# Host-packed channel-major slabs in a hybrid decoder step: wider modulation groups, a first norm in two halves, and small loads behind the first slabs

## The chip, the core and the metric

The kernel runs on one core of one Trainium2 chip. The metric is device time in microseconds (us), the median of the runs shown. The engines are named as in the profile: PE (matmul), PEld (weight load), DVE (vector), ACT (scalar), POOL, and SPq, the queue of the sync engine, which issues every DMA of this kernel in program order.

## The reference, cut to what matters

One layer of a hybrid decoder on 288 tokens (256 of a prompt, 8 samples of 4), model width 1024, everything in float32. A conditioning vector per sequence (9 of them) gives six modulation vectors of 1024 through a 1024 x 6144 weight. The modulated norm feeds two recurrent branches, which are merged, projected and added; a second modulated norm feeds a mixture of experts; a final norm ends it.

```
cs  = silu(c)                                     # (9, 1024)
mod = cs @ w_ada + b_ada                          # (9, 6, 1024)
shift1, scale1, gate1, shift2, scale2, gate2 = mod
h = rms_norm(x, norm1_w) * (1 + scale1) + shift1
proj = h @ w_in                                   # GLA q k v gate, decay rank 16, GDN q k v (conv), z, beta, a, gates
y, new_state_gla, new_state_gdn, new_state_conv = mixer(proj, states)
x = x + gate1 * (y @ w_out)
h = rms_norm(x, norm2_w) * (1 + scale2) + shift2
x = x + gate2 * moe(h)                            # 16 experts, 2 for each token, gate and up 1024x512, down 512x1024
return rms_norm(x, final_norm_w), states
```

## The kernel before, in words

All activations are kept channel-major in one SBUF arena: `xT` and `hT` are 128 partitions x 8 channel blocks x 288 tokens. Each engine runs the same hand-written `schedule` list in order, and takes from each item the part that is its own; engines meet through semaphores. The order of the list is therefore the order of the work on PE, ACT and DVE, and no engine reorders it.

1. **Head.** SPq loads constants (886 KB), the nine conditioning rows, vectors, convolution weights, x in token rows, and a dozen small tensors, and only then the first weight slab. PE turns the rows into channel-major form by transposes (L420 is the line of every matmul, L423 that of every transpose); DVE copies them out.
2. **Modulation.** `w_ada` comes in 24 slabs of 256 columns, 1 MB each. For one slab `ada` does 8 matmuls with 32-column weights and 256 moving columns, in four column groups of the array (four partial sums, two contraction blocks each); ACT copies the bank to `adaq` (L1776), and `fold` adds the four partial sums with two matmuls that have 128-column weights and 9 moving columns; DVE adds the bias (L1038). Slabs 0 to 7 (shift and scale of the first norm) come in the head, and `norm_sums` (the sums of squares of x, 8 matmuls of 288 columns) stands behind the third of them; slabs 8 to 23 stand behind steps 1, 3, ... 31.
3. **First norm and small projections.** `norm` scales and modulates all eight blocks (DVE L1047, L1056 to L1071, ACT L1797). `small` then projects the decay rank, beta and a: 8 matmuls, an ACT copy (L1803), five small matmuls.
4. **Steps 0 to 69.** Step s projects block s of 64 (8 matmuls of 128 x 128 weights and 288 columns), with the transposes, norms and convolution taps of earlier blocks. Weight slabs of 256 columns go through a ring of five 1 MB slots; SPq loads chunk n when chunk n-5 has been used. The pieces of the GLA branch stand at steps 21 to 35 (`GLA_AT`), those of GDN from step 38, and `conv_out` (24 transposes of the convolution tails to token rows) behind step 46.
5. **Output projection, second norm, router, experts.** Eight blocks of two experts each in a loop, whose weights stream from HBM in three 4 MB loads for each block; then the final norm, `y` turned back to token rows by 24 transposes, and four stores.

`ring_bank` hands out four PSUM banks in turn, `take` the other four by number; both wait until the last reader has read.

Of the kernel before, what the change touches and what calls it, by code (L numbers as in the profile page):

```python
# [22 lines left out]
P = 128  # L23
# [55 lines left out]
def constants():  # L79

    p = np.arange(P)
    parts = {"ident": np.eye(P), "ones": np.ones((P, P)), "tri": (p[:, None] <= p[None, :]) * 1.0}
# [10 lines left out]
    parts["eps"] = np.full((P, 1), EPS)  # L93
# [16 lines left out]
CONST, CONST_AT = constants()  # L110

# [37 lines left out]
def _program(nc, ctx, I, O, known):  # L149
# [26 lines left out]
    csT = carve(KD * NC9 + 32 - NC9)  # L176
    adaq = carve(CW)
    vecT = carve(NVEC)
    cst = carve(CONST.shape[1])
    rsB = carve(TOK)  # L180
    rtw = carve(KD * 20 + 12)
    rtb = carve(20)
    gs = carve(2, 32)
# [25 lines left out]
    ccT = carve(CT, 27)  # L209
    wsm = carve(KD, 32)  # L210
    raT_at = top[0]
# [7 lines left out]
    adt = carve(2, HB)  # L219
# [50 lines left out]
    xr = vB  # L270
    cbrow = carve(3072, at=persistent + RING * KD * CW)
    crow = carve(D, at=GB_at)
    csx = carve(2, D, at=vA_at + 0)
    vrow = carve(P, at=GB_at + 1024)
    cvrow = carve(P, at=GB_at + 1152)
    newconv = carve(3072, at=vA_at)

    EW = carve(3, 2, 4096, at=mixer_only)
    yrow = carve(3, D, at=mixer_only)
# [37 lines left out]
    def cols(w, c0, n=CW):  # L317
        return w[:, c0:c0 + n].rearrange("(k p) n -> p k n", p=P)

# [34 lines left out]
    for c in range(8):  # L354
        schedule += [("ada", c)] + ([("fold", c - 1)] if c else [])
        if c == 2:
            schedule.append(("norm_sums", 1))
    schedule += [("fold", 7), ("norm", 1), ("small",)]
    ADA_AT = {ADA_FIRST + ADA_STEP * i: 8 + i for i in range(16)}
    for s in range(NPROJ + 6):  # L360
        schedule.append(("step", s))
        if s == 1:
            schedule.append(("sums",))
# [7 lines left out]
        if s == CONV_OUT_AT:  # L371
            schedule.append(("conv_out",))
    schedule += [("merge",), ("wout",), ("norm_sums", 2), ("norm", 2), ("router",), ("experts",), ("final",)]

    for item in schedule:
        kind, c = item[0], item[-1]
        if kind == "ada":
            add(("ada", c), cols(I["w_ada"], CW * c))
        elif kind == "step" and c % 2 == 0 and c < NPROJ:
            add(("win", c), cols(I["w_in"], PROJ[c][2]))  # L380
        elif item == ("gla_states_read", 2):
            for i in range(4):
                add(("sgla", i), I["state_gla"][2 * i:2 * i + 2].rearrange("s h k v -> k (s h) v"))
        elif item == ("gdn_values", 2):
            for i in range(4):
                add(("sgdn", i), I["state_gdn"][2 * i:2 * i + 2].rearrange("s (h a) k v -> k (s h) a v", a=2))
        elif kind == "wout":
            for i in range(4):
                add(("wout", i), cols(I["w_out"], CW * i))
# [87 lines left out]
    def _(pe):  # L477
        PE[0] = pe

        def head():  # L480
            pe.wait_ge(*when("consts"))
            pe.wait_ge(*when("vec rows"))
            b = ring_bank("vec")
            tr(b[:, 0:NVEC], vrow[0:NVEC, :], NVEC)
            tr(b[:, 128:224], cvrow[0:96, :], 96).then_inc(mark("head_transposed", "vec ready"), 1)
            pe.wait_ge(*when("x rows"))
            for d in range(KD):
                b = ring_bank(f"x{d}")
                for m, (o, n) in enumerate(TILES):
                    last = tr(b[:, o:o + n], xr[0:n, m, 128 * d:128 * d + 128], n)  # L490
                last.then_inc(mark("head_transposed", f"x{d} ready"), 1)
            pe.wait_ge(*when("cb rows"))
            for g in range(2):
                b = ring_bank(f"cb{g}")
                for j in range(12):
                    c = 12 * g + j
                    last = tr(b[:, 24 * j:24 * j + 24], cbrow[0:24, 128 * c:128 * c + 128], 24)
# [1798 lines left out]
```

## Time and profile before

| what | value |
|---|---|
| median of 3 runs (lowest to highest) | 962.63 us (962.33 to 968.43) |
| the profiled execution's own time | 964.75 us |
| its span, first to last instruction | 962.9 us |
| mean granted TensorE clock | 0.959 |
| busy: PE, DVE, ACT, POOL | 871.8, 411.2, 261.2, 66.3 us |
| DMA | 190.64 MB, mean 198 GB/s |

The span is what the trace covers; the execution's own time is 1.9 us longer, and the median of the runs lies 2.1 us below that. A busy PE is not PE at full rate: matmuls overlap, and the granted clock is 1.0 or 0.5 of full speed from one stretch to the next.

### The profile page before, as it was taken

To read this page: it belongs to the slowest core of one execution; us is meant where nothing else is said; L and a number is where in the kernel's file an instruction comes from. 1 tells how busy PE (TensorE), PEld (TensorE's weight loads), DVE (VectorE), ACT (ScalarE), POOL (GpSimd) and SP (SyncE) were. 2 spreads that over 40 slices of the span, in tenths; PEclk is the share of its full clock that TensorE was granted. 3 is DMA by queue.
4 is the path that set the end of the run, shared out by engine and by line. 5 is a ranking of instruction groups with operands and counts; after the bars stand their busy time and mean duration, and the time that the engine had idled before them with its cause. 6 is when DMAs were issued, how large, how long until landed. Compare 5 with 4: busy or idle time off the path is not lost.

```text
span 962.9 us, 13134 instructions
## 1 busy us (share of the span) xinstructions
PE 871.8 (91%) x5070; PEld 611.5 (64%) x5070; DVE 411.2 (43%) x1038; ACT 261.2 (27%) x630; POOL 66.3 (7%) x94
## 2 busy tenths in 40 slices
PE   5889999998979899999999996794999999999994
PEld 3557777676747689878988776573555445554533
DVE  3120004647756865557447447515123222232225
ACT  3121103666732333352433421012101110111012
POOL 1000000000123100000000117310000000000000
PEclk9969999999989999999999998996999999999998
DMA  8947676523517811132113523798399999998811
GB/s 205 349 136 232 203 223 209 176 88 98 168 41 221 261 45 45 47 129 88 45 45 101 145 76 99 211 381 314 116 396 368 384 385 395 376 387 331 292 57 50
DMA packets 134414, 190.64 MB, mean 198 GB/s; under 512 B 6656, under 2 KB 90283, under 8 KB 134309
## 3 DMA queue, kind: packets, MB, share of 16 engines
q1 hardware_dynamic: 134360, 189.89, 58.1%
q8 instruction: 37, 0.61, 0.3%
q14 instruction: 17, 0.14, 0.1%
HBM read 178.93 MB, written 10.95 MB: 197 GB/s over the span
## 4 chain that ended last, share of the span: by engine, by line
PE 79%; DVE 10%; ACT 3%; issue 3%; POOL 2%; SPq 2%; DMA 1%; DVEq 0%; ACTq 0%; POOLq 0%
PE bank L420 76%; PE bank L423 3%; POOL arena L2091 1%; DMA arena<-in_w_ada 1%; DVE arena L1185 1%; DVE arena L1653 1%; DVE arena L1047 1%; SPq L2142 1%; DVE arena L1296 1%; ACT arena L1751 0%; DVE arena L1170 0%; DVE arena L1339 0%; POOL arena L2099 0%; DVE arena L1494 0%; DVE arena L1434 0%
## 5 line engine op out<-in xcount | busy, mean ns | idle before, releaser
L420 PE MATMUL bank<-arena 128*128 128x288 f32 (+9 forms) x4752 | 830.9, 394 | 72.0 <-DVE arena L1071 8.6
L420 PEld LDWEIGHTS bank<-arena 128*128 128x128 f32 (+4 forms) x4752 | 575.5, 172 | 312.1 <-issue 181.0
L1848 ACT ACTIVATE arena<-arena 128x288 f32<-128x288 f32 (+1 forms) x56 | 25.0, 447 | 154.2 <-DVE arena L1170 154.1
L423 PE MATMUL bank<-arena 128*128 128x128 f32 (+6 forms) x318 | 50.3, 291 | 14.9 <-DMA arena<-in_w_conv 7.0
L423 PEld LDWEIGHTS bank<-arena 128*128 128x128 f32 (+6 forms) x318 | 36.9, 149 | 34.5 <-issue 19.8
L1660 DVE TENSOR_TENSOR arena<-arena,bank 128x288 f32<-128x288 f32 x64 | 28.8, 455 | 29.4 <-PE bank L420 28.0
L1185 DVE SCALAR_TENSOR_TENSOR arena<-arena 128x312 f32<-128x312 f32 x72 | 39.4, 548 | 2.5
L1038 DVE TENSOR_TENSOR arena<-bank,arena 128x18 f32<-128x18 f32 x24 | 4.2, 174 | 82.7 <-PE bank L420 82.7
L1640 DVE SCALAR_TENSOR_TENSOR arena<-bank,arena 128x512 f32<-128x512 f32 x8 | 5.5, 693 | 71.4 <-ACT arena L1998 71.4
L1746 ACT ACTIVATE arena<-arena 128x288 f32<-128x288 f32 (+4 forms) x60 | 33.7, 562 | 2.0
L1881 ACT ACTIVATE arena<-bank 128x288 f32<-128x288 f32 x40 | 16.2, 405 | 54.4 <-PE bank L420 30.7
L1321 DVE TENSOR_TENSOR arena<-arena 128x512 f32<-128x512 f32 (+1 forms) x32 | 19.9, 638 | 24.1 <-PE bank L420 24.1
L1170 DVE SCALAR_TENSOR_TENSOR arena<-arena 128x288 f32<-128x288 f32 (+1 forms) x56 | 26.6, 475 | 8.5 <-ACT arena L1746 8.5
L1391 DVE TENSOR_TENSOR arena<-arena,bank 128x512 f32<-128x512 f32 (+1 forms) x26 | 17.0, 657 | 29.5 <-PE bank L420 29.5
L1744 ACT ACTIVATE arena<-arena 128x288 f32<-128x288 f32 (+4 forms) x60 | 28.2, 470 | 1.9
L1751 ACT ACTIVATE arena<-bank,arena 128x288 f32<-128x288 f32 x19 | 9.5, 500 | 68.5 <-PE bank L420 68.5
L1988 ACT ACTIVATE arena<-bank 128x512 f32<-128x512 f32 x8 | 4.8, 599 | 84.4 <-PE bank L420 84.4
L1742 ACT ACTIVATE arena<-arena 128x288 f32<-128x288 f32 (+2 forms) x57 | 25.5, 447 | 4.7 <-DMA arena<-in_cc 3.9
L1994 ACT ACTIVATE arena<-bank 128x512 f32<-128x512 f32 x8 | 4.8, 598 | 80.0 <-PE bank L420 80.0
L2091 POOL TENSOR_SCALAR arena<-arena 128x1024 f32<-128x1024 f32 x8 | 23.3, 2930 | 44.8 <-PE bank L420 44.8
L2056 POOL COPY arena<-arena 128x3 f32<-128x3 f32 x24 | 6.9, 287 | 276.9 <-ACT arena L1876 276.9
L2004 ACT ACTIVATE arena<-bank 128x512 f32<-128x512 f32 x8 | 4.8, 598 | 70.0 <-PE bank L420 70.0
(206 smaller groups left out, 466.8 us busy)
## 6 DMA issues: line engine op xcount, KB each, us to landing
arena<-in_w_in SPq DMA_DIRECT2D x36, 1024.0 KB, 6.6
arena<-in_w_exp_gate SPq DMA_DIRECT2D x8, 4096.0 KB, 14.9
arena<-in_w_exp_up SPq DMA_DIRECT2D x8, 4096.0 KB, 18.2
arena<-in_w_exp_down SPq DMA_DIRECT2D x8, 4096.0 KB, 14.6
arena<-in_w_ada SPq DMA_DIRECT2D x24, 1024.0 KB, 5.3
arena<-in_state_gla SPq DMA_DIRECT2D x4, 1024.0 KB, 6.4
out_gla_s<-arena SPq DMA_DIRECT2D x4, 1024.0 KB, 8.2
arena<-in_w_out SPq DMA_DIRECT2D x4, 1024.0 KB, 6.1
```

The costliest lines, as they stand in the source:

```text
L420: return T.matmul(out, lhsT, rhs, start=start, stop=stop)
L423: return T.transpose(out, in_, ident[0:n, 0:n])
L1170: V.scalar_tensor_tensor(sg, y, 0.0, sg, ALU.min, ALU.subtract) \
L1185: V.scalar_tensor_tensor(y, x[:, j:j + YW], wv(j), y, ALU.mult, ALU.add) \
L1321: V.tensor_tensor(Lm[0:n, hs, 0:n], LT[0:n, hs, 0:n], mid(const(f"level{lv}")[0:n, 0:n], HG), ALU.mult) \
L1391: V.tensor_tensor(X[0:n, hs, 0, 0:n], X[0:n, hs, 0, 0:n], view(6 + g), ALU.subtract) \
L1660: V.tensor_tensor(acc[:, d, :], acc[:, d, :], pm[4 + d % 4][:, 0:TOK], ALU.add).then_inc(n["added"], 1)
L1742: A.activation(dst, src, ACT.Abs).then_inc(mark(kind, event + " abs"), 1)
L1744: A.activation(dst, dst, ACT.Exp, scale=-1.0).then_inc(mark(kind, event + " exp"), 1)
L1746: A.activation(dst, dst, ACT.Ln, bias=one[0:n]).then_inc(mark(kind, event), 1)
L1848: A.activation(sg, sg, ACT.Exp).then_inc(mark("proj_by_scalar", f"sig{s3}"), 1)
L2091: G.tensor_scalar(kem2[:, s % 2, :], ke.rearrange("p a b -> p (a b)"), const("seq")[:, s:s + 1], None, ALU.mult) \
```

## The change

The host now lays every input out as the arena wants it (128 partitions, one contiguous run each), and takes the outputs in that form. On the chip:

- The head's transposes and their copies go, as do `conv_out` and the 24 transposes of `y`; the convolution tails and `y` are stored channel-major. `y` goes out in four stores of two blocks each, as the final scaling produces them.
- The conditioning, the vectors and the constants that the head needs come as one load (`first`, 427 floats in each of 128 partitions), then x; then the weight slabs begin. Four loads (`small`, `later`, `wa2`, `conv`) are issued behind the slab of step 2.
- The modulation is done in 12 groups of 512 columns, each from two 1 MB slabs that hold four contraction blocks each. The four column groups of the array now hold four different blocks of 128 output columns, so nothing is left to add up, and `fold` is one transpose. Groups 2, 0, 3, 1 come in the head (scale and shift of the first half, then of the second), `norm_sums` ahead of them; the other eight behind steps 1, 5, ... 29.
- The first norm is modulated half by half, each when its two groups are there; step 0's matmul k waits for block k. `small` moves from ahead of step 0 to behind step 2, `sums` from step 1 to step 4. The second norm is modulated in halves too, and its scales are formed earlier.
- Three router banks are taken by number; `gla_out` waits for the masked scores.

```diff
-ADA_FIRST, ADA_STEP = 1, 2
+ADA_FIRST, ADA_STEP = 1, 4
-CONV_OUT_AT = 46
+ADA_HEAD = (2, 0, 3, 1)
+ADA_ORDER = ADA_HEAD + tuple(range(4, 12))
+SMALL_AT, SUMS_AT = 2, 4
-NORM_BY_VECTOR = (2, 5)
+NORM_BY_VECTOR = (3, 7)
...
-    for c in range(8):
-        schedule += [("ada", c)] + ([("fold", c - 1)] if c else [])
-        if c == 2:
-            schedule.append(("norm_sums", 1))
-    schedule += [("fold", 7), ("norm", 1), ("small",)]
-    ADA_AT = {ADA_FIRST + ADA_STEP * i: 8 + i for i in range(16)}
+    schedule.append(("norm_sums", 1))
+    for i, c in enumerate(ADA_HEAD):
+        schedule += [("ada", c)] + ([("fold", ADA_HEAD[i - 1])] if i else [])
+        if i == 2:
+            schedule.append(("norm_half", 0))
+    schedule += [("fold", ADA_HEAD[3]), ("norm_half", 1)]
+    ADA_AT = {ADA_FIRST + ADA_STEP * i: 4 + i for i in range(8)}
...
         if kind == "ada":
-            add(("ada", c), cols(I["w_ada"], CW * c))
+            for half in range(2):
+                add(("ada", c, half), I["w_ada"][2 * c + half])
...
         def ada(c):
-            w = slot(("ada", c))
-            b = take(7 - 2 * (c % 2), f"read ada{c}")
-            for k in range(KD):
-                q = k % 4
-                last = mm(b[32 * q:32 * q + 32, 0:CW], csT[:, NC9 * k:NC9 * k + 32], w[:, k, :], k < 4, k >= 4)
+            b = take(7 - 2 * (ADA_ORDER.index(c) % 2), f"read ada{c}")
+            for half in range(2):
+                pe.wait_ge(*when(loaded(("ada", c, half))))
+                w = slot(("ada", c, half)).rearrange("p k n -> p (k n)").rearrange("p (k n) -> p k n", n=512)
+                for j in range(4):
+                    k = 4 * half + j
+                    for q in range(4):
+                        last = mm(b[32 * q:32 * q + 32, 0:P], csT[:, NC9 * k:NC9 * k + 32],
+                                  w[:, j, P * q:P * q + P], k == 0, k == KD - 1)
...
         def fold(c):
-            for j in range(2):
-                last = mm(b[:, NC9 * j:NC9 * j + NC9], adaq[:, 128 * j:128 * j + 128], FOLD[:, 0:NC9])
+            tr(b[:, 0:P], adaq[:, ADA_ORDER.index(c) % 2, :], P).then_inc(mark("ada_products", f"fold{c} ready"), 1)
...
                 for k in range(KD):
+                    if s == 0:
+                        pe.wait_ge(*when(f"h1 {k}"))
+                        pe.wait_ge(*when(f"hp1 {k}"))
                     last = mm(b[:, 0:TOK], w[:, k, 128 * j:128 * j + 128], hT[:, k, :], k == 0, k == KD - 1)
...
         def gla_out(m):
+            pe.wait_ge(*when(t + "AT"))
...
-        def conv_out():
-            for g in range(6):
-                b = ring_bank(f"cvo{g}")
-                for j in range(4):
-                    last = tr(b[0:27, 128 * j:128 * j + 128], ccT[:, 4 * g + j, :], 128)
...
+        def modulate(i, half):
+            dve.wait_ge(*when(f"A{i} {half}"))
+            dve.wait_ge(*when(f"read fold{(base + 4 * half) // 4}"))
+            dve.wait_ge(*when(f"n{i} {4 * half + 3}"))
+            V.tensor_tensor(hs, hs, AA[:, ds, 1:NC9].unsqueeze(3).to_broadcast(wide), ALU.mult)
+            V.tensor_scalar(hT[:, by_vector, 0:SEQ], hT[:, by_vector, 0:SEQ], AA[:, by_vector, 0:1],
+                            modT[:, base + by_vector, 0:1], ALU.mult, ALU.add)
+            V.tensor_tensor(hs, hs, modT[:, base + 4 * half:base + 4 * half + 4, 1:NC9].unsqueeze(3).to_broadcast(wide),
+                            ALU.add)
...
-        load(cst, I["const"], "consts")
-        load(crow[0:NC9, :], I["cc"], "c rows")
...
+        load(arena[:, first_at:first_end], I["first"], "first")
+        load(xT, I["x"], "x")
+        def later_weights():
+            load(arena[:, wsm_at:small_end], I["small"], "small weights")
+            load(arena[:, first_end:later_end], I["later"], "consts")
+            load(wa2[0:RANK + 1, :], I["wa2"], "wa2")
+            load(arena[:, convT_at:convT_at + 96 + CT * 24], I["conv"], "conv weights")
...
+            sp.dma_start(slot(name), src).then_inc(mark(f"loaded_slot{n % RING}", loaded(name), by=16), 16)
+            if name == ("win", 2):
+                later_weights()
...
-            sp.dma_start(into[:, 0:n, :].rearrange("p a (k n) -> p (a k) n", k=4 if kind == 2 else KD),
-                         wts[kind][experts].rearrange("a (k p) n -> p (a k) n", p=P)).then_inc(sem, 16)
+            sp.dma_start(into[:, 0:n, :], wts[kind][experts].rearrange("a p n -> p a n")).then_inc(sem, 16)
...
+        for d in range(0, KD, 2):
+            sp.wait_ge(*when(f"yf {d + 1}"))
+            sp.dma_start(O["y"][:, d:d + 2, :], hT[:, d:d + 2, :]).then_inc(mark("stored", f"y stored {d}", by=16), 16)
```

## Rows read from the trace of the kernel before

**Rows 1.** The page: busy time of PE, and shares of the chain that ended last.
```profile
PE 871.8 (91%) x5070; PEld 611.5 (64%) x5070; DVE 411.2 (43%) x1038; ACT 261.2 (27%) x630; POOL 66.3 (7%) x94
...
PE 79%; DVE 10%; ACT 3%; issue 3%; POOL 2%; SPq 2%; DMA 1%; DVEq 0%; ACTq 0%; POOLq 0%
```

**Rows 2.** Windows: length, busy (instructions) of PE, PEld, DVE, ACT, POOL; clock; DMA share; GB/s.
```profile
100.00:150.00 50.00, 48.33 (x272) 35.40 (x265) 3.14 (x13) 5.71 (x17) 0.33 (x2) 1.00 0.66 210
...
700.00:800.00 100.00, 97.38 (x523) 50.45 (x521) 27.42 (x51) 11.50 (x19) 0.00 (x0) 1.00 1.02 384
```

**Rows 3.** Chain that ended last, 0 to 62 us: start, length, what.
```profile
0.71 0.40 SPq L2123
...
15.78 0.43 SPq L2193
...
54.70 2.63 PE bank L420 x16
```

**Rows 4.** Timeline: PE's and DVE's part in the small projections.
```profile
57.81 17.39 PE L420 MATMUL bank<-arena 128*16 128x288 f32 x80 [0.50 <-ACT arena L1803]
...
60.18 0.19 DVE L1081 COPY arena<-bank 128x32 f32<-128x32 f32 x1 [0.74 <-PE bank L420]
```

**Rows 5.** DMA issues: KB of each, median us from issue to landing.
```profile
arena<-in_const SPq DMA_DIRECT2D x1, 886.0 KB, 4.8
...
arena<-in_gdn_A_log SPq DMA_DIRECT2D x1, 4.0 KB, 2.2
```

**Rows 6.** Windows: the ada loads, clock before step 0, in step 0, expert loads.
```profile
28.00:30.00 2.00, 1.89 (x18) 0.74 (x17) 0.18 (x1) 0.38 (x1) 0.00 (x0) 1.00 1.11 352
44.00:45.00 1.00, 1.00 (x8) 0.93 (x4) 0.00 (x0) 0.00 (x0) 0.00 (x0) 0.50 1.10 347
64.00:65.00 1.00, 1.00 (x5) 0.76 (x4) 0.00 (x0) 0.00 (x0) 0.00 (x0) 0.82 0.00 0
...
650.00:651.00 1.00, 0.00 (x0) 0.00 (x0) 0.96 (x3) 0.01 (x1) 0.00 (x0) 1.00 1.02 406
```

**Rows 7.** PE by form, 28 to 40 us: the sums of squares.
```profile
L420 PE MATMUL bank<-arena 128*128 128x288 f32 x16 | 7.1, 627 | 0.0
```

**Rows 8.** PE by form, 100 to 127 us: projections, ada, fold (two records per matmul).
```profile
L420 PE MATMUL bank<-arena 128*128 128x288 f32 x93 | 24.1, 412 | 0.0
L420 PE MATMUL bank<-arena 128*32 128x256 f32 x48 | 3.2, 384 | 0.0
L420 PE MATMUL bank<-arena 128*128 128x9 f32 x12 | 1.5, 236 | 0.0
```

**Rows 9.** Chain at 561.7 us: 128 matmuls, 32-column weights, 128 columns.
```profile
561.70 7.17 PE bank L420 x256
```

**Rows 10.** PE timeline: a fold that waits for ACT; a GLA step.
```profile
134.58 4.59 PE L420 MATMUL bank<-arena 128*128 128x9 f32 x20 [0.83 <-ACT arena L1776]
...
183.62 1.07 PE L420 MATMUL bank<-arena 128*32 128x256 f32 x16 [0.35 <-DVE arena L1220]
186.75 1.59 PE L420 MATMUL bank<-arena 128*128 128x128 f32 x8 [2.05 <-DVE arena L1237]
```

**Rows 11.** Window behind that GLA step.
```profile
188.00:190.00 2.00, 2.00 (x9) 1.71 (x9) 1.93 (x7) 1.28 (x4) 0.00 (x0) 0.50 1.08 351
```

**Rows 12.** PE by form, whole span: the transposes of the convolution tails.
```profile
L423 PE MATMUL bank<-arena 128*27 128x128 f32 x24 | 2.8, 271 | 0.0
```

**Rows 13.** Chain, second norm: eight products on DVE, then the router's matmuls.
```profile
650.04 3.04 DVE arena L1047 x8
...
655.16 2.48 PE bank L420 x16
```

**Rows 14.** Timeline, the end: eight final scalings, the last store's issue.
```profile
952.05 3.52 DVE L1722 SCALAR_TENSOR_TENSOR arena<-arena 128x288 f32<-128x288 f32 x8 [4.44 <-ACT arena L1755]
...
959.84 0.47 SPq L2250 DMA_DIRECT2D out_y_s<-arena  x1
```

**Rows 15.** PE by form, whole span: gate, up and down products, and their waits.
```profile
L420 PE MATMUL bank<-arena 128*64 128x512 f32 x768 | 172.0, 599 | 7.0 <-DVE arena L1653 7.0
```

More of the change, by code:

```diff
@@ L478, in _ @@
         PE[0] = pe
[L480 to L497, printed above, removed]
-                last.then_inc(mark("head_transposed", f"cb{g} ready"), 1)
-            b = ring_bank("c")
-            for k in range(KD):
-                last = tr(b[:, NC9 * k:NC9 * k + NC9], crow[0:NC9, 128 * k:128 * k + 128], NC9)
-            last.then_inc(mark("head_transposed", "c ready"), 1)
@@ new lines, in ada @@
+            for half in range(2):
[6 more added lines that the diff above has]
+                                  w[:, j, P * q:P * q + P], k == 0, k == KD - 1)
+                last.then_inc(mark("ada_products", used(("ada", c, half)), *([f"ada{c} ready"] if half else [])), 1)
@@ L861, in router @@
         def router():
-            pe.wait_ge(*when("router weights"))
-            pe.wait_ge(*when("router padding"))
+            pe.wait_ge(*when("consts"))
             b = ring_bank("router parts")
@@ L901, in router @@
             q = MORE * NE
-            b = ring_bank("over")
+            b = take(7, "read over")
             mm(b[0:q, 0:1], tri[0:q, 0:q], over[0:q, 0:1])
@@ L967, in experts @@
             pe.wait_ge(*when("one-hot"))
-            b = ring_bank("table")
+            b = take(5, "read table")
             q = MORE * NE
@@ L1074, in small, with norm_half @@
+        def norm_half(half):
+            scales(1, half)
+            modulate(1, half)
+        def norm(i):
+            for half in range(2):
+                for d in range(4 * half, 4 * half + 4):
+                    normed(2, d)
+                modulate(2, half)
         def small():
+            dve.wait_ge(*when("consts"))
             dve.wait_ge(*when("ra ready"))
@@ L1079, in small @@
             dve.wait_ge(*when("ba ready"))
-            dve.wait_ge(*when("adt"))
+            dve.wait_ge(*when("small weights"))
             V.tensor_copy(ba[:, 0:2, :], rb("ba")[:, 0:32].rearrange("p (a b) -> p a b", b=16))
@@ L1176, in step @@
                     x, y = xp[:, s1 % 2], yb[:, s1 % 4]
-                    dve.wait_ge(*when("read c"))
+                    dve.wait_ge(*when("conv weights"))
                     for event in y_free(s1 - 4):
@@ L1520, in wout @@
         def wout():
[L1521 removed]
+            dve.wait_ge(*when("read fold5"))
             for d in range(KD):
@@ L1799, in norm, with norm_half @@
                     .then_inc(mark("norm_by_scalar", f"hp{i} {d}"), 1)
+        def norm_half(half):
+            modulate(1, half)
+        def norm(i):
+            for half in range(2):
+                modulate(2, half)
         def small():
+            act.wait_ge(*when("consts"))
             act.wait_ge(*when("small parts ready"))
@@ L1869, in step @@
                     act.wait_ge(*when("xp zero"))
-                    act.wait_ge(*when("read cb1"))
+                    act.wait_ge(*when("conv weights"))
                     if i >= 2:
@@ L2026, in final @@
             rstd(rsB, rb("norm3")[:, 0:TOK], 1.0 / D, "norm_by_scalar", "rstd3", mid_event="read norm3")
-            for g in range(2):
-                act.wait_ge(*when(f"y{g}1 ready"))
-                A.activation(yrow[:, 1, 512 * g:512 * g + 512], rb(f"y{g}1")[:, :], ACT.Copy) \
-                    .then_inc(mark("final_by_scalar", f"read y{g}1"), 1)
         run(locals())
```

320 lines of the change are left out of this document (126 added, 194 removed).

## The prediction

> **What bounds the kernel now.** I read the page first: PE is busy 91% of the span and makes up 79% of the chain that ended last, DVE 10%, DMA 1% [rows 1]. That is an average, so the windows by stage come next. Between 100 and 150 us PE is busy 48.3 of 50 us and in the experts 97.4 of 100, at full clock in both [rows 2]: there a microsecond taken off PE is a microsecond of the span, and nothing else is. The head is different. The chain in order of time shows that the first slab of modulation weights is issued only at 15.8 us, behind everything SPq had to issue before it, although its first issue stands at 0.7; after the ada groups come the small projections, and step 0 starts when the last small product is out, at 60.2 us [rows 3, 4]. So the change can pay in three kinds: an earlier step 0, PE work taken out of the dense steps, and a shorter end.
>
> **The head: when step 0 starts afterwards.** First the loads. A 886 KB load landed 4.8 us after its issue and a 4 KB one 2.2 us [rows 5]; `first` is 219 KB, so by proportion 2.8 us, landing at 3.5. x (1.18 MB) and eight slabs (1.05 MB each) follow without a gap. The rate is the unknown: 352 GB/s for slabs in runs of 1 KB, 406 for expert weights in runs of 2 and 4 KB [rows 6]. At these two rates x lands at 6.9 or 6.4, a slab takes 2.98 or 2.58 us, the eighth lands at 30.7 or 27.0 and the ninth, step 0's own, at 33.7 or 29.6. The new runs are 8 KB, so I take the higher rate, whose row is nearer, and keep the other for the range.
>
> The Trainium skill, "DMA: Bandwidth & Descriptors", section Specifications, gives about 358 GB/s as the limit of HBM for one core; by that the eight slabs would take 23.4 us in place of 20.6 and the sum below would come out 2.8 us later. The 406 of the expert row is above that figure, so the row stands.
>
> The ring holds five slabs: the sixth is issued when the first half of the first group has been used, and that stands behind `norm_sums` on PE. `norm_sums` took 7.1 us for 16 records, 0.44 each, where the same form takes 24.1/93 = 0.26 later [rows 7, 8]: PE runs at or near its half level here (1.2 of 2.4 GHz), whatever the clock column says before its first change. From 6.9 it ends near 14.0. A group's first half is then 16 matmuls; of this shape (32-column weights, 128 columns) 256 records took 7.17 us, 0.028 each [rows 9], so a group (64 records) costs 1.8 us at the full level, 3.6 at half. The sixth slab is issued near 16, when the fifth still has three microseconds to go: no gap. Four groups at half level and their folds end near 29.5, the copy and the last transpose of the bank near 30; the loads alone would allow 27.0 + 1.8 + 0.7 = 29.5 (0.7 is an estimate: a copy like the one that PE waits 0.50 us for [rows 4], and a transpose). Both limits meet, and I take **31 us** for step 0 (29.5 if the clock rises early, 34 at the lower rate). The modulation of the second half, 1.1 to 2.1 us on DVE and ACT (half to all of what lies between the products' end and the router in the second norm [rows 13]), lies beside step 0's first four matmuls, which use the first half; if it took over 3.6 us PE would wait by the excess.
>
> Two things are paid back. `small` took from 54.7 to 60.2, 5.5 us at half level [rows 3, 4, 6], of which 0.5 is PE's wait for an ACT copy [rows 4]; behind step 2 at the full level it costs 5.0/2 + 0.5 = 3.0. DVE and ACT, which work for it, have little queued in steps 2 to 4. And step 0 starts at the half level: before, it ran so until 64.4 (the mean of 0.82 in that microsecond) [rows 6], 4.2 us, a loss of 2.1. PE had then worked without a break since 57.8 [rows 4], 6.6 us. Afterwards it has worked on and off before step 0, so I take 6 us of step 0 at half, a loss of 3.0. The head gives 60.2 - 31 - 3.0 - 0.9 = **25.3 us**, with bounds of 21 and 28.
>
> The four late loads move past the ring on SPq without a wait; they delay the slab of step 4 by 1.4 MB, 3.4 to 3.9 us. The two that `small` needs land at 40 to 46, when four more slabs are in; PE comes to `small` near 31 + 3 x 4.1 (16 records of 0.26) + 3.0 + 1.9 = 48. A miss costs what it is late by, and everything behind it on PE.
>
> **Modulation in the steps.** Before, 256 columns cost 3.2/3 = 1.07 us of ada and 1.5/3 = 0.5 of fold [rows 8], 16 times: 25.1. Twice the fold also waited 0.83 for ACT, which is held up by the transposes of earlier blocks [rows 10]: 1.7, and one of the two remains. After, eight groups at 1.8, and eight folds of one transpose, 2.8/24 = 0.12 [rows 12]: 15.4. That is 10.6 gross. But PE is not the bound everywhere: in the GLA step at 183 us ada stood in a stall, PE waiting 2.05 us for DVE right behind it [rows 10]. That slot, and those four and eight steps later, lose their ada; nothing is gained there, so 3 x 1.07 comes off. Net **7.4 us**, bounds 3 and 11: the lower if the GLA chains take up what the folds free.
>
> A rule that speaks against 64 short records for a group in place of 32 longer ones is in the Trainium skill, "TensorE: Matmul & The Clock Gate", section "Wait — 56ns, not 53.3ns?": without hardware decode the sequencer spends about 62 ns on each matmul. What it would do here is the third rival. The 0.028 us for a record says that it doesn't bind.
>
> **Convolution tails.** 24 transposes, 2.8 us [rows 12], in a dense stretch: **2.8**, or nothing if the next GDN step would wait for DVE instead. The tails are stored by DMA as they stand, beside the matmuls.
>
> **Second norm.** The products start at 650.0 and the router's matmuls at 655.2, which take 2.5 us [rows 13]. In halves DVE does the same work, but half the router products can run before the last block is there: half of 2.5, **1.2 us**; bounds 0 and 2. The waits added to `gla_out` and the renumbered banks are for results that are long there by the order of the list; I cost them at nothing, and a step of PE at most if not.
>
> **The end.** The last scaling ends at 952.05 + 3.52 = 955.6, and the last store can be issued then rather than at 959.8 [rows 14]. It is 295 KB in place of 64, at 406 GB/s 0.6 us more: 4.2 - 0.6 = **3.6 us**, bounds 3 and 4.2.
>
> Sum: 25.3 + 7.4 + 2.8 + 1.2 + 3.6 = 40.3. The profiled execution's own 964.75 becomes 924.5, and as it lies 2.1 above the median of the runs, **922 us**. The bounds alone give 912 to 931.
>
> **Rivals.**
> *The GLA chains and the clock take the steps' gain.* Behind the stall at 183 us the clock is at half at 188 [rows 11]. Without ada in the slot PE stands still there for about 3.5 us at a stretch, and the slots four and eight steps later may get such a fall too. Each lasts about 6 us, so 3 us lost, 6 in all; with the steps' gain down to 3 the time is 922 + 4.4 + 6 = 932. For it: the rows of the first slot. Against: the clock falls there anyway.
>
> *More than forecast.* The clock rises in the head and stays, falls elsewhere shift away, and all 10.6 us come: 922 - 3 - 3 - 3 = 913.
>
> *The short records bind.* 64 records at 62 ns are 4.0 us for a group in place of 1.8: eight times 2.2 is 17, time 939. This is the rule of the Trainium skill's TensorE page named above, with each record taken as one instruction. The row of 0.028 us [rows 9] speaks against it.
>
> *Slower: the expert loads in 16 KB runs.* A block of two experts takes 12.6 MB, at 384 GB/s 32.8 us, and the DMA engines are at a share of 1.02 there [rows 2]. If long runs were slower than the old ones, PE would wait in each of eight blocks. At 352 GB/s a block takes 35.7 us, 24 more in all, 946; below 333 GB/s (37.8 us) the whole gain is gone, and at 320 the time is 974. Against it: the releaser of the expert products is DVE alone, never a load [rows 15], so there is some slack, and a rate under the 352 of 1 KB runs is shown nowhere.
>
> *The loads don't come as meant.* Were x or the sixth slab 4 us late, the head would give 21, and the time be 926: inside the forecast's bounds.
>
> **How the numbers follow.** Forecast 0.75 (with the loads' case), GLA and clock 0.11, more than forecast 0.07, short records 0.02, slower 0.03, something between 937 and 953 0.02. The range that leaves out no more than 2 in 10, with the bounds of the costs and the first two rivals: 910 to 936. One per cent, 9.6 us, is about what a measurement of this kernel can tell from no change; all cases but the slower one and half of the one before it lie more than that below 962.6: faster 0.95, same 0.02, slower 0.03.
>
> **What would show it.** Right: step 0's first matmul between 29 and 34 us, slabs landing every 2.6 us from about 9; a group near 1.8 us in the steps and no wait for ACT except once; no transposes at step 46; the last store issued right behind the scalings. Wrong: PE waiting for a load in the experts; new stretches at half clock behind steps 27 and 31; `small` waiting for its weights; ada records near 60 ns.

## The result, and the profile afterwards

The changed kernel takes **927.85 us** (median of 4 runs, 923.67 to 930.42); the kernel before, beside it, 963.74 (962.33 to 968.43). The ratio is **0.9615**, interval [0.9565, 0.9666]. Five more runs of the same file, beside other kernels, gave 927.38 and 0.9631 [0.9602, 0.9659]. The forecast was 922, the range 910 to 936. The profiled execution took 928.78 us by its own time and has a span of 927.0; the comparisons of rows below are made with this span and the 962.9 of before. One run of all that follow, 977.27 us of a variant of the kernel before, lies more than 1.5% above that variant's fastest and is left out of its median.

The page of the changed kernel (busy time; shares of the chain that ended last; the DMA issues), against [rows 1, 5]:

```profile
PE 840.9 (91%) x5264; PEld 597.2 (64%) x5264; DVE 396.7 (43%) x981; ACT 251.3 (27%) x616; POOL 67.1 (7%) x92
...
PE 80%; DVE 9%; ACT 4%; DMA 3%; issue 2%; POOL 1%; SPq 0%; DVEq 0%; ACTq 0%; POOLq 0%
...
arena<-in_w_in SPq DMA_DIRECT2D x36, 1024.0 KB, 5.1
```

PE's share of the chain has hardly moved, but DMA now has 3% of it in place of 1%: that is the head. The chain in order of time from the first instruction, against [rows 3]:

```profile
3.18 13.19 DMA arena<-in_w_ada
...
16.41 1.08 PE bank L420 x32
...
17.55 12.60 DMA arena<-in_w_in
...
30.20 15.14 PE bank L420 x128
```

Step 0 starts at 30.2, where it started at 60.2, and two stretches of loading (13.19 and 12.60 us) fill most of what lies in front of it. The windows of the head and of the two dense stretches (columns as in [rows 2]):

```profile
8.00:20.00 12.00, 8.87 (x144) 6.72 (x142) 3.24 (x9) 2.73 (x8) 0.00 (x0) 1.00 1.01 424
20.00:24.00 4.00, 3.00 (x56) 2.50 (x60) 0.00 (x0) 0.00 (x0) 0.00 (x0) 0.57 1.01 422
24.00:30.00 6.00, 3.40 (x83) 2.21 (x74) 1.58 (x8) 2.14 (x5) 0.00 (x0) 1.00 1.01 418
30.00:45.00 15.00, 14.80 (x128) 11.06 (x128) 0.85 (x4) 3.09 (x7) 0.00 (x0) 1.00 1.02 411
...
118.00:150.00 32.00, 32.00 (x254) 24.74 (x251) 18.88 (x50) 17.49 (x50) 2.41 (x12) 1.00 0.64 230
700.00:800.00 100.00, 97.37 (x522) 50.47 (x522) 27.47 (x52) 11.33 (x18) 0.00 (x0) 1.00 0.94 387
```

The DMA engines are busy without a break from 8 us on, at 411 to 424 GB/s, and PE's clock is full (1.00) in step 0, where it was at half before [rows 6]. The experts are as they were: 97.37 of 100 us, and no wait for a load.

PE's timeline in the GLA steps, against [rows 10]; in the brackets the wait ahead of a group and who ended it:

```profile
154.11 2.04 PE L420 MATMUL bank<-arena 128*128 128x128 f32 x8 [3.81 <-DVE arena L1205]
...
173.48 7.30 PE L420 MATMUL bank<-arena 17*128 17x512 f32 x20 [1.24 <-DVE arena L1269]
...
189.95 1.13 PE L420 MATMUL bank<-arena 128*128 128x128 f32 x8 [3.81 <-DVE arena L1205]
...
211.04 0.63 PE L423 MATMUL bank<-arena 128*128 128x128 f32 x4 [1.44 <-ACT arena L1732]
...
253.85 8.38 PE L420 MATMUL bank<-arena 128*128 128x256 f32 x23 [5.00 <-DVE arena L1264]
```

Where PE waited 0.35 + 2.05 us ahead of the scores before, it now waits 3.81, twice. The next view decides most of what follows. It takes one and the same stretch in four profiles, from the transposes in step 17 to the start of the 5.0 us wait above: before, after, the second profile of the changed kernel (`r_after_again`) and the first improvement below (`e5`).

```profile
150.18:279.31 129.13, 121.09 (x683) 87.54 (x681) 78.28 (x202) 79.09 (x228) 11.72 (x36) 0.97 0.44 139
```
```profile
117.75:248.85 131.10, 119.01 (x783) 88.37 (x781) 78.09 (x198) 77.56 (x224) 11.45 (x36) 0.96 0.37 137
```
```profile
118.31:254.07 135.76, 121.98 (x783) 90.72 (x781) 78.09 (x198) 77.57 (x224) 11.44 (x36) 0.94 0.36 132
```
```profile
117.65:240.62 122.97, 114.57 (x783) 84.80 (x781) 77.81 (x198) 77.75 (x224) 11.46 (x36) 1.00 0.39 146
```

This stretch holds half of the modulation groups, and the change was to shorten it. It is 2.0 us *longer* in the first profile after and 6.6 in the second. PE's idle time (length less busy) was 8.0 before and is 12.1 and 13.8 after; the clock went from 0.97 to 0.96 and 0.94.

The second norm and the end, against [rows 13, 14]:

```profile
623.56 1.03 PE L420 MATMUL bank<-arena 128*32 128x288 f32 x8 [3.82 <-DVE arena L1027]
625.78 1.50 PE L420 MATMUL bank<-arena 128*32 128x288 f32 x8 [1.19 <-DVE arena L1027]
...
913.80 6.07 PE L420 MATMUL bank<-arena 128*128 128x288 f32 x16 [3.50 <-ACT arena L1987]
...
920.92 3.52 DVE L1684 SCALAR_TENSOR_TENSOR arena<-arena 128x288 f32<-128x288 f32 x8 [2.66 <-ACT arena L1711]
...
921.89 2.91 SPq L2170 DMA_DIRECT2D out_y<-arena  x4
```

### The profile page after: what moved, and what is told of

The parts are those of the page before. It is cut to its first block, busy times and chain, and to the rows that moved or that the text cites. A ratio compares the mean times of both kernels' runs of the same rounds, so it can differ in the third digit from the quotient of the medians.

```text
span 927.0 us, 13353 instructions
## 1 busy us (share of the span) xinstructions
PE 840.9 (91%) x5264; PEld 597.2 (64%) x5264; DVE 396.7 (43%) x981; ACT 251.3 (27%) x616; POOL 67.1 (7%) x92
## 4 chain that ended last, share of the span: by engine, by line
PE 80%; DVE 9%; ACT 4%; DMA 3%; issue 2%; POOL 1%; SPq 0%; DVEq 0%; ACTq 0%; POOLq 0%
PE bank L420 78%; PE bank L423 2%; DMA arena<-in_w_ada 1%; DMA arena<-in_w_in 1%; POOL arena L2048 1%; DVE arena L1153 1%; DVE arena L1615 1%; ACT arena L1707 1%; DVE arena L1301 0%; DVE arena L1264 0%; DVE arena L1138 0%; DVE arena L1684 0%; DVE arena L992 0%; DVE arena L1456 0%; ACT arena L1700 0%
## 5 line engine op out<-in xcount | busy, mean ns | idle before, releaser
L420 PE MATMUL bank<-arena 128*128 128x288 f32 (+10 forms) x5040 | 814.1, 376 | 75.2 <-DVE arena L1205 8.6
L423 PE MATMUL bank<-arena 128*128 128x128 f32 (+2 forms) x224 | 38.2, 292 | 3.8 <-ACT arena L1732 2.5
L423 PEld LDWEIGHTS bank<-arena 128*128 128x128 f32 (+2 forms) x224 | 26.8, 143 | 20.3 <-issue 10.1
L986 DVE TENSOR_TENSOR arena<-bank,arena 128x36 f32<-128x36 f32 x12 | 2.3, 192 | 45.1 <-PE bank L423 45.0
```

The source lines that it names most:

```text
L420: return T.matmul(out, lhsT, rhs, start=start, stop=stop)
L423: return T.transpose(out, in_, ident[0:n, 0:n])
```

## The experiments

Three theories stood at the start. *The theory*: the head is set by the bytes ahead of step 0's slab; the gain in the steps was lost because groups that had filled PE's waits ahead of the GLA scores were moved out of them. *Rival one*: a group costs more than forecast, wherever it stands. *Rival two*: the place does not matter, DVE and ACT bound those steps whatever PE does in between. All edits but one are made to the changed kernel. "Lost to the clock" is the sum of (1 - granted clock) over windows of 1 us.

**Groups in front of the scores.**

```
-    ADA_AT = {ADA_FIRST + ADA_STEP * i: 4 + i for i in range(8)}
+    ADA_AT = {1: 4, 5: 5, 9: 6, 13: 7, 23: 8, 25: 9, 27: 10, 31: 11}
```

> Four of the eight modulation groups that stand in the steps move from steps 17, 21, 25 and 29 to 23, 25, 27 and 31, so that three of them stand just ahead of the GLA scores, where PE waits 3.81, 3.81 and 0.96 us for DVE in the changed kernel. Theory (the steps' gain was lost because the change took the groups out of these stalls): the stalls shrink to about 1.7, 1.7 and 0, that is 2.1 + 2.1 + 0.9 = 5 us, and if the fall of the clock at 190 us goes with them another 2; 4 to 8 us less than the changed kernel, 920 to 924. Rival (a group simply costs more than forecast wherever it stands): the span is that of the changed kernel within 1 us, the waits for DVE move back by what PE gains.

Measured: 930.74 (928.33 to 932.59), ratio 0.9659 [0.9627, 0.969]: no gain. The timeline of PE, ACT and DVE shows why:

```profile
150.38 1.13 PE L420 MATMUL bank<-arena 128*128 128x128 f32 x8 [1.63 <-DVE arena L1205]
...
154.63 0.68 DVE L1221 TENSOR_TENSOR arena<-bank,arena 128x512 f32<-128x512 f32 x1
...
154.98 0.28 ACT L1732 ACTIVATE arena<-bank 128x128 f32<-128x128 f32 x1
...
155.40 1.08 PE L423 MATMUL bank<-arena 128*128 128x128 f32 x4 [3.89 <-DVE arena L1221]
```

The wait for DVE did shrink, 3.81 to 1.63, but right behind it there is a new one of 3.89, here and four steps later. The view names DVE, which had nothing that these transposes read; the copy of the group on ACT (L1732) ends at 155.26, just ahead of them. The group had been given bank 7, which the transposes of the keys write next, and its copy stands on ACT behind the whole work of the step. The theory's first half was right, and my placement made a new wait: the run does not tell the rivals apart.

**Late loads in front again.**

```
+        later_weights()
         for n, (name, src) in enumerate(chunks):
 ...
-            if name == ("win", 2):
-                later_weights()
```

> The four late loads (1.39 MB) are issued again right behind first and x, ahead of all slabs; nothing else changes. Theory (the head is paced by the bytes ahead of step 0's slab at the 418 GB/s of the trace): step 0 starts 1.39/0.418 = 3.3 us later, near 33.5, and the end comes 3 to 3.5 us later than in the changed kernel. Rival (PE's chain of groups and folds sets step 0, as the prediction had it as the second of two limits): step 0 within 0.7 us of 30.2, no change of the end.

Measured: 930.87 (930.12 to 931.84), ratio 0.9666 [0.964, 0.9691]. The small projections come 4.2 us later (50.06 in place of 45.88 for the row below), the span ends 1.3 later, the median is 3 later.

```profile
50.06 1.37 PE L420 MATMUL bank<-arena 128*16 128x288 f32 x8 [0.59 <-ACT arena L1768]
```

The bytes set the head: between 13 and 32 us PE waits for a slab ahead of each half group. The 4.2 are more than the 3.3 that 1.39 MB take at the rate of the slabs. Step 0 starts at 34.14, 3.9 later, and not behind a wait for its slab: the clock is at half from 31 to 35 us here, and the last half group takes 1.89 us in place of 1.08. So the loads set the pace, and at the very end PE's chain is close behind them.

**The first norm in one go.** `norm_half(0)` is put behind the last fold.

> The first norm is modulated in one go behind the last fold instead of in two halves. Theory (the slab of step 0 lands at 30.2, the last fold is read at 29.9): the first half takes DVE and ACT about 1 us more before step 0's first matmul, the second half 1 to 1.5 us after it; step 0 starts 0.5 to 1.5 us later and its end is 1 to 2 us later; the end likewise. Rival (the landing of the slab hides it, as the loads are the limit): step 0's end within 0.3 us of the changed kernel.

Measured: 929.85 (929.11 to 936.49), ratio 0.9675 [0.9631, 0.9718], by the times not to be told from the changed kernel. Step 0's first matmul:

```profile
30.89 16.53 PE L418 MATMUL bank<-arena 128*128 128x288 f32 x128 [1.29 <-DVE arena L996]
```

It starts 0.7 later, and PE waits for DVE in place of the slab. So the halves are worth 0.7 us, little, because the slab lands at 30.2 anyway. The 128 records take 16.5 in place of 15.1 because the clock is at half from 30 to 34 us here; that belongs to the run as much as to the edit (the second profile of the unaltered kernel has such a fall from 20 to 32 us).

**Each group in the steps multiplied twice.**

```
-            for half in range(2):
+            for half in (0, 1) if c in ADA_HEAD else (0, 1, 2, 3):
+                again, half = half < 2 and c not in ADA_HEAD, half % 2
 ...
+                if again:
+                    continue
```

> Each of the eight groups in the steps is multiplied twice over (the second pass overwrites the first). Theory (none of the eight stands in a stall now, a group costs PE 2.0 to 2.1 us): 16 to 17 us over the changed kernel, 944. Rival one (short records bind at about 62 ns): 32 us over it, 960. Rival two (the groups are still covered by waits): under 10 us over it.

Measured: 936.9 (934.66 to 937.42), ratio 0.9717 [0.9689, 0.9745]: 9 us over the changed kernel, not the 16 to 17 of the theory.

```profile
164.66 1.13 PE L420 MATMUL bank<-arena 128*128 128x128 f32 x8 [3.80 <-DVE arena L1208]
```

This row is the 154.11 of after: 10.55 later, of which 1.83 were there at the small projections (47.71 against 45.88). Five groups lie in between (steps 5, 9, ... 21), so a second pass costs 8.7/5 = **1.74 us**. From there on the shift hardly grows (10.77 at the 5.0 us wait): the second passes of the last two groups come out of waits (1.24 becomes 0.44, 1.44 becomes 0.34) and of a fall of the clock that does not come (174 to 178 us in the first profile after). So six of the eight passes are paid and two are covered, and the 2.2 us between this shift and the spans (935.6 and 927.0) are given back behind the steps. The first of the rivals named above is out: a group costs about what was forecast, 1.8.

**The same once more.** The file of the changed kernel, unaltered.

> The changed kernel once more, unaltered, beside the three that follow. If the falls of the clock at 542 to 560 and 624 to 649 us (8.5 and 11.9 us lost in the first profile, 5.1 and 10.2 in the three kernels that were edited elsewhere) are a matter of where the kernel's stretches happen to lie, this profile has them there again or in another size, and the times scatter over 923 to 931 as before; if they belong to the change, they stand in the same places at the same size.

Measured: 927.38 (924.41 to 929.9). The small products behind the last projections, in the first profile and in this one:

```profile
540.97 11.01 PE L420 MATMUL bank<-arena 32*32 32x128 f32 x56 [0.29 <-DVE arena L1396]
```
```profile
545.94 8.36 PE L420 MATMUL bank<-arena 32*32 32x128 f32 x56 [0.29 <-DVE arena L1396]
```

The same 56 records, the same waits around them, 11.0 and 8.4 us. In the first profile the clock is at half from 542 to 560 (8.5 us lost), in this one from 546 to 550 and from 556 to 564 (5.1 lost). In exchange this one lost 3.4 more in the head and 1.7 more each in the steps at 154 to 161 and 242 to 247, and the spans are 927.0 and 928.1. So the falls have places where they tend to come, but their size is settled anew in each execution; a stretch of one profile can be 4 to 5 us off for that alone.

**Groups in front of the scores, in the other bank.**

```
-    ADA_AT = {ADA_FIRST + ADA_STEP * i: 4 + i for i in range(8)}
+    ADA_AT = {1: 4, 5: 5, 9: 6, 13: 7, 17: 8, 23: 9, 25: 10, 27: 11}
```

Against the changed kernel two groups move, from step 21 to 23 and from 29 to 27. The banks alternate with the group's number, so the groups of steps 23 and 27 now get bank 5, as they had in the changed kernel.

> As the first experiment, but the groups ahead of the GLA scores (steps 23 and 27) write the bank that the transposes of the keys do not use; there the first experiment had a new wait of 3.89 us behind each, because the copy of the group stood behind a step's work on ACT. Theory (the groups fill the stalls, the shared bank gave it back): PE waits at most 2.5 us at each of the two places in all, the new waits of 3.9 are gone, GDN starts 3 to 5 us earlier than in the changed kernel and the end comes 3 to 7 us earlier, 921 to 925. Rival (the chain of DVE and ACT in these steps is the bound whatever PE has in between): GDN starts within 1 us of the changed kernel.

Measured: **917.25** (916.96 to 919.82), ratio 0.9536 [0.9512, 0.9561], beside 0.9631 for the changed kernel measured next to it: 10 us less, more than the 3 to 7 expected.

```profile
152.73 1.13 PE L420 MATMUL bank<-arena 128*128 128x128 f32 x8 [1.22 <-DVE arena L1205]
...
185.91 1.13 PE L420 MATMUL bank<-arena 128*128 128x128 f32 x8 [1.22 <-DVE arena L1205]
...
245.62 21.50 PE L420 MATMUL bank<-arena 128*128 128x256 f32 x74 [5.00 <-DVE arena L1264]
```

The waits are 1.22 in place of 3.81, and no wait of 3.9 stands behind them. The last of the four windows above is this kernel's: the same work, x783 as after, in 122.97 us in place of 131.10 and 135.76. PE's idle time is 8.4, and the clock is 1.00 throughout, where the two profiles of the changed kernel have three and four falls. The second of the rivals named above is out. Of the 8.1 us against the first profile 3.7 are idle time and the remaining 4.4 are busy time, the same instructions at full clock: in this pair of profiles more than half of what the filling gives comes back through the clock. Once more beside its neighbours:

> The version with groups ahead of the GLA scores and the other bank, once more beside its neighbours: 915 to 920, ratio 0.951 to 0.956, no fall of the clock between 30 and 240 us. If its 917 was a lucky set of falls, 922 to 926.

Measured: 918.5 (916.02 to 921.37), ratio 0.9551 [0.9529, 0.9573], again no fall between 32 and 246 us. It was not luck.

**One step more between sums and scores.** All groups ahead of step 19; the GLA parts of tiles 0 and 1 are spread over one step more:

```
-GLA_AT = ((21, 22, 23, 23, 24, 25), (25, 26, 27, 27, 28, 29), (29, 30, 31, 33, 34, 35))
+GLA_AT = ((19, 20, 22, 22, 23, 24), (24, 25, 27, 27, 28, 29), (29, 30, 31, 33, 34, 35))
-    ADA_AT = {ADA_FIRST + ADA_STEP * i: 4 + i for i in range(8)}
+    ADA_AT = {1: 4, 4: 5, 7: 6, 9: 7, 12: 8, 14: 9, 16: 10, 18: 11}
```

> All eight groups stand ahead of step 19, and tiles 0 and 1 of GLA get one step more between sums and scores (tile 0 two steps earlier, tile 1 one step earlier at its start), so that 3.9 us of projection stand where PE waits 3.81 us for DVE. Theory (these waits are the room that the old groups filled): both waits go to under 0.5, the falls of the clock behind them with them; 6 to 9 us before GDN starts, end 918 to 923. Rival (DVE and ACT bound those steps): the waits come back elsewhere before step 38 and the end stays within 2 us of the changed kernel.

Measured: 921.87 (919.91 to 923.71), ratio 0.9584 [0.9559, 0.9608]. That is inside the 918 to 923 expected. The waits for DVE ahead of the scores of the first two tiles are gone and the clock falls once in these steps (171 to 175 us), but two other waits have grown, the second of them for ACT and just ahead of the second tile's scores:

```profile
170.54 16.44 PE L420 MATMUL bank<-arena 17*128 17x512 f32 x62 [2.83 <-DVE arena L1269]
...
189.44 1.64 PE L420 MATMUL bank<-arena 128*128 128x288 f32 x10 [2.47 <-ACT arena L1805]
```

Better than the changed kernel, not as good as filling the waits with work that has to be done anyway.

**The kernel before, its groups moved.** The mirror of it, in the kernel before: four of the 16 groups, three of them from in front of the scores, go to earlier, dense steps. One wait for the scores ahead of the GLA products is written out.

```
-    ADA_AT = {ADA_FIRST + ADA_STEP * i: 8 + i for i in range(16)}
+    ADA_AT = dict(zip((1, 2, 3, 5, 6, 7, 9, 10, 11, 13, 14, 15, 17, 21, 25, 29), range(8, 24)))
 ...
+            pe.wait_ge(*when(t + "AT"))
```

> The kernel before, with only its modulation groups of 256 columns moved: those of steps 19, 23, 27 and 31 go to steps in front of step 18 (16 groups in steps 1, 2, 3, 5, 6, 7, 9, 10, 11, 13, 14, 15, 17, 21, 25, 29), and one wait for the scores is written out in front of the GLA products. No work is added or removed. Theory (groups in front of the GLA scores are free, anywhere else they are paid, and the waits that they leave behind let the clock fall): three groups are paid that were free (3 x 1.6), the waits for DVE at the scores of tiles 0 and 1 grow from 2.4 to 3.8 us, and there is a new fall of the clock behind step 27; 4 to 8 us slower than the kernel before, ratio 1.004 to 1.008. Rival (the place of the groups does not matter): ratio 0.998 to 1.002.

Measured: 965.89 (962.8 to 974.3, 11 runs) against 962.15 (17 runs), ratio **1.0039** [1.0015, 1.0064]: a little slower with the same work, 3.7 us where 4 to 8 were expected. The runs scatter over 11.5 us, more than the effect, and the profiled execution is the longest of them (974.3), so mainly its waits are read:

```profile
190.04 2.05 PE L420 MATMUL bank<-arena 128*128 128x128 f32 x8 [3.48 <-DVE arena L1238]
...
226.01 1.13 PE L420 MATMUL bank<-arena 128*128 128x128 f32 x8 [3.47 <-DVE arena L1238]
```

PE waits 3.48 where the kernel before has 0.35 + 2.05 around a group of 1.07: these add up to 3.47, so the group stood wholly inside the wait and taking it away gained nothing there. The clock also falls from 227 to 231 and from 247 to 255 us, where the kernel before has no fall; that the shorter executions have these falls too is not shown. This is the same kind of loss as in the changed kernel, made without its other edits.

**Filling waits with matmuls that nobody reads.** Three versions: in the late stretch of the changed kernel (32 matmuls in the last GDN tile and ahead of the output projection, 12 in the second norm), then in the first improvement, once in front of the 5.0 us wait and once in the late stretch.

```
+        def fill(count):
+            n = len(ring_names)
+            pe.wait_ge(*when(f"read {ring_names[n - 4]}"))
+            for _ in range(count):
+                mm(pm[n % 4][:, 384:512], ident, tri)
 ...
```

> Matmuls whose result nobody reads are put ahead of PE's waits between 537 and 626 us of the changed kernel (2 ahead of 0.6, 9 ahead of 3.96, 2 ahead of each 0.77, 11 ahead of 4.64, 9 ahead of 3.82, 3 ahead of 1.19), at 0.27 us each at full clock and twice that at half. Theory (the clock falls there because PE stands still now and then): the stretches at half between 540 and 650 become fewer, 17.5 us are lost in them now; 4 to 10 us less than the changed kernel, 918 to 924. Rival (the falls have another reason, such as the small products between the waits): the falls stay as they are, and the added matmuls cost 0 to 3 us.

> That version, with 12 matmuls whose result nobody reads (0.27 us each at full clock) ahead of the wait of 5.0 us in front of the second sampled GLA state, where the clock fell for 8 us in its profile. Theory (the clock falls because PE stands still): no fall there, 2 to 3 us less than that version. Rival (the matmuls take as long as they save, or the fall comes anyway): within 1 us of it. If the first matmul behind the expert loop again waits 5.5 us in place of 3.5, as in the kernel with the late fills and in the kernel before, 2 us are given back there.

> That version with the late fills of the earlier experiment (537 to 626 us). Theory: the experts start 3 to 5 us earlier; if the first matmul behind the expert loop waits 3.5 us, the end comes 3 to 5 us earlier, 912 to 914; if it waits 5.5 us as it did with the late fills alone, 1 to 3 us earlier. Rival: no gain within 1 us, as the falls move elsewhere.

Measured: 924.82 (923.38 to 929.08), 0.9613 [0.9584, 0.9643], for the first: not to be told from the changed kernel beside it. 920.08, 0.9555 [0.9528, 0.9582], and 919.51, 0.9546 [0.9525, 0.9567], for the others: the same as the improvement without them (0.9551). All three fell short of the gain that their theory expected. PE in the first of them, and ahead of the second GLA state in the second:

```profile
639.70 15.68 PE L420 MATMUL bank<-arena 32*128 32x8 f32 x84 [1.43 <-DVE arena L1651]
...
912.14 7.06 PE L420 MATMUL bank<-arena 128*128 128x288 f32 x16 [5.49 <-ACT arena L1999]
```
```profile
246.24 20.57 PE L420 MATMUL bank<-arena 128*128 128x256 f32 x74 [2.33 <-DVE arena L1272]
```

In the late stretch the fills do what they were to do: between 540 and 650 us 11.9 us are lost to the clock in place of 23.8 and 17.0 in the two profiles of the changed kernel, and the row with which the experts begin (639.70) comes 99.2 us behind the start of that tile's last chain (540.49), against 103.7 and 101.4. Then it is given back: from there to the end it takes 286.6 us against 283.6 and 282.1. Two of these are the first matmul of the last norm, which waits 5.49 us in place of 3.50, and the rest the clock in the last sums. In front of the 5.0 us wait the fills only change its name: PE waits 2.33 in place of 5.00, but DVE ends the wait at 246.2 with or without them (246.21 in the improvement's second profile), and the clock falls at 246 in both. A matmul that nobody reads gained nothing at this wait, whose end another engine sets.

## Why the prediction came out as it did

The time lies in the range, 6 us above the forecast; the sign and the main term were right. The sum promised 40.3 us of the span, the two spans differ by 35.9. That it came so near is in part luck: the head, the tails and the end gave 6.3 more than forecast, the other terms about 11 less. The prediction's "912 to 931" from the bounds alone is a slip of its sum: its bounds add up to 27 us, with the tails and the second norm at nothing, and to 48, which is 936 to 915; the range that it stated covers both. Term by term, from the rows of the profiles:

| Term | Forecast | Measured |
|---|---|---|
| Head, small projections paid | 25.3 | 28.6 |
| Modulation in the steps | 7.4 | 1.8 |
| Convolution tails | 2.8 | 3.2 |
| GDN, last tile | 0 | -4.4 |
| Second norm and router | 1.2 | 0.15 |
| End | 3.6 | 6.2 |

**The head** was sized 3.3 us too small. The copy of step 0 (ACT, before and after) moves from 66.36 to 34.38, 32.0:

```profile
66.36 0.41 ACT L1862 ACTIVATE arena<-bank 128x288 f32<-128x288 f32 x1 [4.13 <-PE bank L420]
```
```profile
34.38 0.41 ACT L1827 ACTIVATE arena<-bank 128x288 f32<-128x288 f32 x1 [2.73 <-PE bank L420]
```

The small projections behind step 2 cost 3.3 where 3.0 was forecast (the copies of steps 2 and 3 lie 7.22 apart, those of steps 0 and 1 3.88). Step 0 starts at 30.2 where I had 31, and it runs at the full level, where I had charged it 3.0 for half. Of the two limits that the prediction saw meet, PE's chain at half level and the loads, the loads ended last, as PE had only short work between them (8.87 of 12 us busy from 8 to 20 us). The rate was 411 to 424 GB/s against 406 taken. The sentence on the limit of HBM for one core (the Trainium skill, "DMA: Bandwidth & Descriptors", section Specifications, about 358 GB/s) does not hold for this stretch: the measurement decides.

**Modulation in the steps is the term that failed**, and the step of it is this: "That slot, and those four and eight steps later, lose their ada; nothing is gained there, so 3 x 1.07 comes off." The emptied slots were priced at nothing gained, and the clock behind them at nothing; they cost more. The price of a group was near: 1.74 us for a second pass against 1.8, 0.027 us a record, and 2.1 in its place (the copies of steps 1 and 2 lie 5.96 apart, those of steps 0 and 1 3.88). The 62 ns of the Trainium skill ("TensorE: Matmul & The Clock Gate", section "Wait — 56ns, not 53.3ns?") would have made the doubling cost 4.0 each with every record counted, as the third rival did, and 2.0 counted by matmul, which is how the page states it; the 1.74 us measured are 54 ns for each of 32 matmuls, below either. Up to step 17 the groups gave 3.8 us where 5.7 were to be had (eight old ones at 1.57 and their waits of 1.7, less four at 1.9 and one wait of 0.8): three waits for ACT (0.73, 0.65, 0.65) stand there where one of 0.83 was forecast, which is 1.2 of the 1.9 missing; no run tests why they are there. From step 17 to the 5.0 us wait they gave -2.0 (-6.6 in the second profile). PE's idle time grew by 4.05, most of which the 3 x 1.07 had priced; what had no term is the clock, which lost 5.1 us in this stretch against 3.4 before, and 8.5 in the second profile, where PE also waits 2.51 us at 241 for nothing that the view names. Moving two groups back in front of the scores gives 10 us; moving four away in the kernel before, three of them from in front of the scores, costs 3.7. That settles it against both rivals of the experiments; how the loss divides between waits and clock rests on two executions that differ.

The prediction had this as its first rival, at 0.11: GLA chains and clock take the steps' gain, 932. It is the mechanism that came true; the time lies between it and the forecast because the head gave more and the end too. In the second profile the steps reach about what that rival gave them. Its size of a fall was too large: they last 4 to 5 us in these steps and cost 1.7 each, where it had 6 and 3. My argument against it, "the clock falls there anyway", read one fall where the question was how many would follow.

**The convolution tails** gave 3.2 against 2.8 (333.67 to 415.71 before, 303.23 to 382.09 after).

**The last GDN tile** was not touched by the change and was not forecast. Of its 4.4 us, 3.1 are the fall at 542 to 560 us, 1.4 in the second profile. The other 1.2 come with a wait amid the 256 records of [rows 9]:

```profile
534.13 2.35 PE L420 MATMUL bank<-arena 128*32 128x128 f32 x74 [0.89 <-issue]
```

All twelve profiles with the new layout have such a wait in these records (0.6 to 1.6 us, for nothing that the profile shows), and neither profile of the old one has it. So it comes with the change; its cause stays open.

**The second norm** was right at its own place: from the end of the output projection to the end of the router's products it takes 7.55 us in place of 8.61, 1.1 against 1.2. Behind it the router ran at half (624 to 649 us) and gave 0.9 back.

**The end** gave 4.8 by the stores, from the start of the last scalings to the end of the span less the same before ((962.9 - 952.05) - (927.0 - 920.92)), against 3.6; the larger store was cheap. The other 1.4 lie ahead of it and were not forecast: the sums of the last norm start right behind the first square, 6.78 us after the last block's additions begin in place of 8.63 (1.85, less 0.45 for the slower clock in the sums).

**The remaining rivals.** Short records: out, as above. Slower expert loads: a block of two experts takes 32.6 us in all profiles, and the expert products wait for DVE alone, as in [rows 15]:

```profile
L420 PE MATMUL bank<-arena 128*64 128x512 f32 x768 | 172.0, 599 | 7.0 <-DVE arena L1615 7.0
```

Of the signs named ahead, "new stretches at half clock behind steps 27 and 31" came: 191 to 195 us, behind step 27. And "no wait for ACT except once" did not hold: there are three up to step 17.

## What to carry to other kernels

Before work is taken out of a stretch or moved, look what stands right behind each piece: a piece in front of a wait that another engine ends can cost nothing where it is, and taking it away leaves a longer wait and perhaps a slower clock behind it. Work that has to be done anyway and can be done at any time belongs in front of such waits, in a bank and behind a copy that nobody there needs next; the place of two groups was worth 10 us here, over a quarter of what the whole change gave.

Judge an edit of a few us by several runs, and by the waits in the rows, not by the length of one stretch in one profile.

## What the runs showed that was not expected

- The same instructions behind the same waits took 11.0 us in one execution and 8.4 in another, as the clock fell for 18 us or for two shorter stretches. In the stretches at 542 and 624 us PE was busy 14.0 of 18 and 17.0 of 25 us; the fall also covers work that runs without a wait.
- A wait can be put down to an engine that has nothing to do with it: the 3.89 us that the view gives to DVE end 0.14 us after ACT's copy out of the bank that PE writes next.
- The first matmul behind the experts' loop waits 3.5 us in ten of the profiles and 5.3 to 5.5 in four others: the kernel before, its variant, and the two with late fills. More instructions on PE alone do not do it (the doubled groups, 256 matmuls more, wait 3.50). What does stays open; it is worth 2 us at the end.
